# Second mixer's output for tokens 0-127 first, cross attention of tokens 128-255 behind the first key scores

## The reference

```python
x = x + merged @ w_out[l]                                  # "wo2"
h = rmsnorm(x, norm_xa_g[l]); m = rmsnorm(mem, norm_mem_g[l])
x = x + memory_cross_attention(h, m, xa_w_q[l], xa_w_kv[l], xa_w_o[l])   # "xq", "xo"; 4 heads of 128, 256 memory rows
h = rmsnorm(x, norm_ffn_g[l])
x = x + peer_ffn(h, peer_w_q[l], peer_subkeys[l], peer_w_down[l], peer_w_up[l])   # "pq", experts
return rmsnorm(x, final_g)
```

## Time and profile before

| | us |
|---|---|
| median of 3 runs | 1304.25 |
| lowest, highest | 1302.63, 1304.44 |
| span of the profiled execution | 1302.2 |
| median less that span | 2.05 |
| TensorE busy | 1188.0 (91%) |
| VectorE busy | 920.6 (71%) |
| ScalarE busy | 545.5 (42%) |
| first gather issued | 642.48 |

### The profile page before, as it was taken

The page is one execution under the profiler, slowest core; times in us unless marked ns, Lnnn a source line. Parts: engine busy times, 40 slices in busy tenths (PEclk is TensorE's granted clock), DMA queues, the critical chain, the costliest instruction groups (busy, mean ns, idle before and its releaser), DMA issues.

```text
span 1302.2 us, 16734 instructions
## 1 busy us (share of the span) xinstructions
PE 1188.0 (91%) x5950; PEld 845.7 (65%) x5950; DVE 920.6 (71%) x1836; ACT 545.5 (42%) x983; POOL 285.0 (22%) x261
## 2 busy tenths in 40 slices
PE   9999999999999999999999889999777877777776
PEld 9998999888888999998865545545322332332322
DVE  6885858777854865567797777776767777777655
ACT  5833655566533547536643333322322222222312
POOL 0000000000000000000145455443643444544420
PEclk9999999999999999999999999999999999989999
DMA  7544456455655654456799999999999999999996
GB/s 287 194 166 148 167 200 213 169 178 183 225 195 194 213 176 160 164 196 230 318 408 402 420 419 420 419 420 419 420 420 418 421 419 422 419 422 419 420 420 262
DMA packets 55925, 396.67 MB, mean 305 GB/s; under 512 B 6320, under 2 KB 6320, under 8 KB 8624
## 3 DMA queue, kind: packets, MB, share of 16 engines
q0 software_dynamic: 36864, 268.45, 49.9%
q1 hardware_dynamic: 17136, 119.16, 25.6%
q10 hardware_dynamic: 1856, 8.13, 1.8%
HBM read 394.67 MB, written 1.05 MB: 304 GB/s over the span
## 4 chain that ended last, share of the span: by engine, by line
PE 56%; DMA 31%; DVE 6%; issue 3%; ACT 3%; POOL 2%; DVEq 0%; POOLq 0%; ACTq 0%
DMA R<-experts,IDX 31%; PE ps L606 19%; PE ps L707 10%; PE ps L1190 8%; PE ps L926 4%; PE ps L654 3%; PE ps L928 2%; POOL R L2778 2%; PE ps L618 2%; DVE R L2564 2%; PE ps L674 1%; PE ps L1041 1%; PE ps L1095 1%; ACT DIAG L1645 1%; PE ps L1068 1%
## 5 line engine op out<-in xcount | busy, mean ns | idle before, releaser
L1190 PE MATMUL ps<-R,DIAG 128*128 128x512 f32 x1020 | 484.6, 623 | 102.7 <-ACT DIAG L1645 97.5
L1190 PEld LDWEIGHTS ps<-R,DIAG 128*128 128x128 f32 x1020 | 191.5, 197 | 371.3 <-issue 206.9
L2564 DVE CUSTOM_DVE_ANT_0 R<-R,XN 128x1024 f32<-128x1024 f32 x256 | 313.4, 1227 | 143.5 <-DMA R<-experts,IDX 137.8
L2778 POOL DMA_INDIRECT R<-experts,IDX x256 | 283.7, 1108 | 535.4 <-PE ps L1190 278.4
L1774 DVE TENSOR_TENSOR w_lo<-raw,w_hi 128x1024 fp32r<-128x1024 f32 x204 | 241.7, 1220 | 89.3 <-ACT w_hi L1243 84.9
L1243 ACT ACTIVATE w_hi<-raw 128x1024 fp32r<-128x1024 f32 x203 | 204.7, 1051 | 78.0 <-DMA raw<-weights 78.0
L1633 ACT ACTIVATE act_d<-dots,rst 128x2 f32<-128x2 f32 (+1 forms) x130 | 38.5, 296 | 329.4 <-DVE dots L2564 329.2
L1645 ACT ACTIVATE DIAG<-con,coef 128x128 f32<-128x128 f32 x255 | 88.6, 394 | 121.3 <-DVE coef L2573 118.1
L606 PE MATMUL ps<-both_C,w_hi 128*128 128x256 f32 x576 | 105.3, 284 | 0.3 <-ACT GA L1277 0.3
L2758 POOL TENSOR_SCALAR_AFFINE_SELECT WS<-WS 128x1024 f32<-128x1024 f32 x1 | 1.1, 1085 | 439.0 <-DMA BS<-gbs 439.0
L606 PEld LDWEIGHTS ps<-both_C,w_hi 128*128 128x128 f32 x576 | 90.3, 192 | 1.4 <-issue 0.8
(11 more groups left out here) (407 smaller groups left out, 1734.2 us busy)
## 6 DMA issues: line engine op xcount, KB each, us to landing
raw<-weights SPq DMA_DIRECT2D x103, 1024.0 KB, 4.8
PQW<-weights SPq DMA_DIRECT2D x6, 1024.0 KB, 9.4
R<-experts,IDX POOLq DMA_INDIRECT x256, 31.8
LNR<-rows ACTq DMA_DIRECT2D x3, 1024.0 KB, 4.7
raw<-weights SPq DMA_DIRECT2D x4, 512.0 KB, 8.4
XF<-xT SPq DMA_DIRECT2D x2, 512.0 KB, 5.6
MEM<-mem ACTq DMA_DIRECT2D x1, 1024.0 KB, 5.0
XR<-x ACTq DMA_DIRECT2D x1, 1024.0 KB, 7.8
```

The costliest lines, as they stand in the source:

```text
L1190: mm = pe.matmul(psum[:, 4 + 2 * m + n, :], DIAG[:, k, :], rows_[:, D + n * 512:D + (n + 1) * 512], start=(it % 8 == 0 and k == 0), stop=True,
L2564: dve.tensor_tensor_reduce(out=rows_[:, 0:D], in0=rows_[:, 0:D], in1=XN[:, m, :], scale=1.0, scalar=0.0, op0=ALU.mult, op1=ALU.add, accum_ ...
L2778: pool.indirect_dma_start(out=R[u][:, :], out_offset=None, in_=experts, in_offset=bass.IndirectOffsetOnAxis(ap=IDX[:, it, k:k + 1], axis=0 ...
```

## The change

What it does, part by part:

- **wo2.** Its first two blocks are loaded early into free buffers and split there, so that all four blocks lie in SBUF at once. TensorE computes both column halves for tokens 0-127 first (`wo2_rows`), and tokens 128-255 in pieces (`second`) between the steps of the first half's cross attention.
- **Norms.** The rows are transposed without the gain; the evacuation from PSUM multiplies by it. The root mean square of the cross attention's norm goes into the scale of the softmax's exponential. The second half's query is computed in its transposed form.
- **Cross output of tokens 0-127.** Its second block is computed in two groups of 256 columns.
- **Cross attention of tokens 128-255** starts behind `head_scores(0, 0)`. Its query and its output are plain fp32 matmuls on weights that are loaded a second time (`XQB`, `XOB`).
- **Queries.** All eight `pq` blocks have buffers of their own; the first query is written in two banks and evacuated in two pieces.
- **Buffers.** The first eight gathers have other buffers, opened by other events. VectorE, before the first dots, has the gains of half 0 and the second half's softmax; the residuals of half 1 come in the first pass, with waits for the cross output.

```diff
-        OPENED = {0: (11, None), 1: (18, None), 2: (8, VALUES_END)}
...
+        OPENED = {0: (18, ("xo_a", 3)), 1: (6, ("xo_a", 3)), 2: (2, ("xo_a", 3)), 3: (11, ("xq_b", 1)),
+                  4: (12, ("xq_b", 1)), 5: (8, ("values", 1)), 6: (1, ("xo_b", 2)), 7: (5, ("xo_b", 2))}
...
+            load(ma + 1, slot_of(ma + 1), half_end(ma - 3))
+            whole(early_raw[0], wo2, early_in[0])
+            load(gm, slot_of(gm), half_end(ma - 2))
+            sp.wait_ge(gm_ready, 2)
+            whole(early_raw[1], wo2 + 1, early_in[1])
...
             sp.wait_ge(m2_ready, 4)
...
+            for j in range(3):
+                whole(PQW[j], PQ0 + j, pq_in[j])
+            sp.wait_ge(xq_a, 1)
+            load(xo, slot_of(xo))
+            sp.wait_ge(xq_a, 2)
+            load(xo + 1, slot_of(xo + 1))
+            sp.wait_ge(gemm_done, half_end(wo2))
+            whole(XQB[0], xq, xqb_in[0])
+            sp.wait_ge(gemm_done, half_end(wo2 + 3))
+            whole(XQB[1], xq + 1, xqb_in[1])
+            for j in range(3, 8):
+                whole(PQW[j], PQ0 + j, pq_in[j])
+            sp.wait_ge(xo_a, 1)
+            for g in range(2):
+                whole(XOB[g], xo + g, xob_in[g])
...
+            def cross_query_second():
...
+                for h in range(XH):
+                    for k in range(DC):
...
+                        mm = pe.matmul(bank(r)[:, h * P:(h + 1) * P],
+                                       XQB[k // 4][:, at_, (h % 2) * P:(h % 2 + 1) * P], H3B[:, k, :],
+                                       start=(h == 0 and k == 0), stop=(k == 7), skip_group_check=True)
+                mm.then_inc(xq_b, 1)
...
+            def cross_out_second(g):
+
+                pe.wait_ge(xob_in[g], 16)
+                for i in range(4):
+                    mm = pe.matmul(psum[:, 6 + g, :], AXB[:, i, :],
+                                   XOB[g][:, 2 * i:2 * i + 2, :].rearrange("p a b -> p (a b)"),
+                                   start=(i == 0), stop=(i == 3), skip_group_check=True)
+                mm.then_inc(xo_b, 1)
...
+            turn("h3Tc", 0, "wo2", 4, XR, 1, range(4, 8))
+            head_scores(0, 0)
+            cross_query_second()
             cross_scores(1, 0)
             cross_scores(1, 1)
-            turn_side("h4Ta", 1, 0, 1, 6)
-            query(0, 0)
+            query(1, 0)
             cross_turn(1, 0)
-            head_scores(0, 0)
             cross_turn(1, 1)
-            query(1, 0, (0,))
             cross_values(1)
-            query(1, 0, (1,))
             head_scores(1, 0)
-            has_lo(pe, *values_parts(1))
-            side("xo", AXo, 0, 1)
-            side("xo", AXo, 1, 1)
-            query(2, 0)
+            query(2, 0, (0,))
+            wait_aux(pe, "xpvb")
+            cross_out_second(0)
+            cross_out_second(1)
+            query(2, 0, (1,))
             query(3, 0, (0,))
             head_scores(2, 0)
...
             first_eight()
-            values_lo(1)
             inverse_side(3, 0)
+            dve.wait_ge(rows2_in, 16)
+            gain_side(0, first_cols)
+            gain_side(0, last_cols)
             second_eight()
+            cross_max(1, 0)
+            cross_max(1, 1)
             top_h(0)
-
+            cross_weights(1, 0)
+            cross_weights(1, 1)
+            dve.wait_ge(xn_gain, 2)
+            dot_rows(0, 0)
             top_a(1)
-            top_b(1)
-            dot_rows(0, 0)
-            residual_side("xo", 3, 1, 0)
             coefs(0, 0)
             dot_rows(0, 1)
-            residual_side("xo", 4, 1, 1)
+            top_b(1)
             coefs(0, 1)
-            gain_side(1, 1, 0)
-            gain_side(1, 1, 1)
+            residual_side("xo", 4, 1, first_cols)
+            residual_side("xo", 5, 1, last_cols)
+            gain_side(1, first_cols)
+            gain_side(1, last_cols)
             top_c(1)
             dot_rows(0, 2)
```

More of the change, by code:

```diff
@@ L69, in half_end, with slot_of, split_end @@
     return 2 * b + h + 1
+EARLY = (BLOCK["wo2"], BLOCK["wo2"] + 1)
+SLOT = {BLOCK["wo2"] + 2: 3, BLOCK["wo2"] + 3: 0, BLOCK["xq"]: 1, BLOCK["xq"] + 1: 2, BLOCK["xo"]: 1,
+        BLOCK["xo"] + 1: 2}
+LOADED = {}
+for _n in range(BLOCK["wo2"]):
+    LOADED[_n] = _n // 4 + 1
+for _n, _s in SLOT.items():
+    LOADED[_n] = 1 + max(v for b, v in LOADED.items() if SLOT.get(b, b % 4) == _s)
+def slot_of(b):
+    return SLOT.get(b, b % 4)
+def split_end(b, h=1):
+    return half_end(b if b < BLOCK["wo2"] else b - 2, h)
 def group_end(stage, j):
@@ L659, in by_rows, with query_part @@
                             mm.then_inc(gemm_done, 1)
+            def query_part(j, m, c, ks):
+                r = RING["pq"] + QUERIES.index((j, m))
+                apart = (j, m) == (0, 0) and c == 1
+                dst = bank(r + 1 if apart else r)[:, c * P:(c + 1) * P]
+                for k in ks:
+                    mm = pe.matmul(dst, PQW[j][:, k, c * P:(c + 1) * P], H4[m][:, k, :],
+                                   start=((c == 0 or apart) and k == 0), stop=(k == 7), skip_group_check=True)
+                return mm
@@ new lines, in wo2_rows @@
+            def wo2_rows(g, m, i):
+                k, h = i // 4, i % 4 // 2
+                w = wo2_weights(g, k, h)
+                if m == 0:
+                    has_lo(pe, "m2", i // 2)
+                for n, (a, o) in enumerate(parts(w, opC)):
+                    mm = pe.matmul(psum[:, 4 + 2 * m + g, :], o[:, i, m * P:(m + 1) * P],
+                                   a[:, 2 * (i % 4):2 * (i % 4) + 2, :].rearrange("p a b -> p (a b)"),
+                                   start=(i == 0 and n == 0), stop=(i == 7 and n == 2), skip_group_check=True)
+                if m == 0 and i == 7:
+                    mm.then_inc(wo2_a, 1)
+                elif m and i % 2:
+                    mm.then_inc(gemm_done, 1)
@@ new lines, in _, with second, turn @@
+            second_rows = iter([(g, i) for g in range(2) for i in range(8)])
+            def second(count):
+                for _ in range(count):
+                    g, i = next(second_rows)
+                    wo2_rows(g, 1, i)
+            def turn(name, j, stage, n, src, m, chunks):
+                dst = free_aux(name, j)
+                wait_wide(pe, stage, n)
+                for n_, c in enumerate(chunks):
+                    mm = pe.transpose(dst[:, n_ * P:(n_ + 1) * P], src[:, m, c * P:(c + 1) * P], ident)
+                mm.then_inc(aux_done, 1)
@@ L1150, in _ @@
+            turn("h3Ta", 0, "wo2", 1, XR, 0, range(4))
+            for i in range(4, 8):
+                wo2_rows(1, 0, i)
+            cross_query(0, 0)
+            turn("h3Ta", 1, "wo2", 2, XR, 0, range(4, 8))
+            cross_query(0, 1)
+            cross_query(1, 0)
+            cross_query(1, 1)
+            second(1)
+            wait_drained(pe, "xq", 0)
+            transposes("qTa", 0, [QN[:, h * P:(h + 1) * P] for h in range(XH)])
+            second(1)
             cross_scores(0, 0)
@@ L1264, in ahead @@
             def ahead(b):
-                while split_to[0] < min(b, BLOCK["pq"] - 1):
+                while split_to[0] < min(b, BLOCK["wo2"] - 1):
                     split_to[0] += 1
@@ L2604, in _ @@
             coefs(0, 4)
-            rows_across("h4Tb", 1)
+            rows_across(1)
             top_h(1)
```

636 lines of the change are left out of this document (323 added, 313 removed).

## The result

The changed kernel takes 1311.19 us (median of 5 runs, 1310.72 to 1312.79) against 1304.25 before: ratio 1.0063, 95% interval 1.0052 to 1.0073, so slower by 0.5 to 0.7%. Forecast were 1310.5 us and "slower". The profiled execution has a span of 1309.0 us against 1302.2.

A forecast was written before the change was run, and what follows sets the result against it. TensorE was taken to bound the kernel up to the first sum, the gathers' transfers after it. Work +3.0 and waits +3.9 us delay that sum; between +4.4 and +7.8, +6.3 was taken: 1304.25 to 1310.5 us, range 1301.5 to 1314.0.

The forecast's parts named there:

- The bound: TensorE bounds up to the first sum; gathers at 420 GB/s later carry a delay at about 700 us to the end.
- Early projections cost nothing: Before the first sum: early wo2 split, reordered residuals and gains in evacuations cost nothing, hidden on VectorE and ScalarE.
- First gather: Work removed ahead of the first key scores, 8.1 us, moves the first gather from 642.48 to about 634.4 us.
- TensorE's work: Before the first sum: fp32 cross query +1.87, cross output +1.44, half-width groups +0.15, query transposes -0.45; sum +3.0 us.
- TensorE's waits: Second half's cross attention, a chain through three engines: 5.4 us of waits against 1.5 idle before, +3.9 us.
- First sum and ninth gather: First sum at 665.7 us; ninth gather waits for the second sum, issued at 669.6, landing +7.8 us later.
- The hole: After five gathers in flight and the sixth at about 652 us, the DMA idles some 8 us before later gathers.
- the gathers never dry up: Rival, faster: buffers six to nine free before the DMA empties at 655 us; about -5.5, 1298.7 us; chance 0.13.
- So TensorE sets the pace again: Behind the ninth gather, up to the 24th: TensorE sets the pace, +6.9 us; DMA's possible return makes +4.4 at most.
- The table loads: ScalarE's three table reloads before the fifth sum's diagonals, 1.78 us of TensorE's idle time, would recur 6.9 us later.
- TensorE doesn't wait: Rival, no change: handovers hide, first sum at 661.8 us, end moves +0.5 to 1304.8 us; chance 0.2.
- Starves longer: Rival, slower still: pass 0's dots and diagonals queue behind late residuals, DMA loses another 3 us; +9.5, 1313.7 us; chance 0.17.

The follow-up runs named there:

- b_more_pe: Kernel before plus eight plain fp32 matmuls of 512 columns ahead of the second half's cross output: 1311.85 us, ratio 1.0063.
- a_again: The changed kernel unaltered, measured a second time in another group of runs: 1313.25 us, ratio 1.0081.
- a_weights_first: Changed kernel with VectorE's two products of the second softmax ahead of the last part of the first pick list: 1311.23 us, ratio 1.0054.
- a_sum_best: Changed kernel with the first two sums around the second cross output's second half and VectorE's softmax weights earlier: 1311.58 us, ratio 1.0058.
- b_sum_first: Kernel before with the first sum ahead of a query and key scores, its VectorE products and ScalarE diagonals also earlier: 1307.8 us, ratio 1.0030.
- a_tables_early: Changed kernel with ScalarE's square root and next gate's exponential, hence the table loads, ahead of the fourth activation: 1311.18 us, ratio 1.0061.
- a_waits_out: Changed kernel with softmax products, last normed chunks and half a query earlier, first two gather buffers exchanged: 1310.41 us, ratio 1.0055.
- a_sum_first: Changed kernel with the first sum directly behind the second half's cross output, ahead of two queries and key scores: 1312.74 us, ratio 1.0071.
- b_tables: Kernel before with ScalarE's gelu and diagonals of the fifth pair ahead of its table reloads: 1304.94 us, ratio 1.0014.

## Why the prediction was right, point by point

**The bound.** Right in kind. The transfers behind 720 us run at 420 GB/s in both kernels, so a delay at 700 us is kept, and the delay comes from TensorE. b_more_pe shows that work on TensorE alone makes such a delay. The forecast calls TensorE the bound up to the first sum; in the kernel before the chain of waits runs through VectorE from 640.50 to 671.12 us, but for 0.3 us of ScalarE, so VectorE is about as near to being the bound there.

**Early projections cost nothing.** Nearly. In front of the first key scores TensorE waits 0.65 us for H3A's low part and 0.17 for the query's, counted in the forecast as 0.5 for "small ones". That the projections' order is otherwise free was read from the trace only; no experiment undid it.

**First gather.** Forecast 634.4, measured 632.73 and 634.59 (a_again). Both are 48.2 and 50.3 us behind the start of the second projection, which itself shifts by up to 2.0 us from one execution to another, in kernels of either order; I take no part of it for the change.

**TensorE's work.** Forecast +3.0 us, and its terms hold: the second cross query takes 7.38 us with its tail (forecast 7.3 and the tail), the second cross output 6.87 (forecast 6.88). The busy time of the stretch grew by 4.8 us, and the rest of it, 1.8 us, was not forecast: the same 16 matmuls of the values take 3.25 us in the changed kernel and 1.95 before, and the four of the key scores 1.06 and not 0.6, at half the clock.

**TensorE's waits.** Forecast 5.4 us (its terms add up to 5.5), measured 5.58. One by one: normed rows 0.98 (1.2), cross query's copy 0.84 (0.8), softmax weights 1.83 and none (1.8 and 0.4), copy of the turned weights 0.89 (0.8), small ones 0.82 (0.5), with 0.2 left over. a_weights_first shows that the 1.8 were VectorE's order.

**First sum and ninth gather.** Forecast 665.7 and 669.6; measured 666.24 and 670.61 (668.10 and 672.47 in a_again). The first figure profits from an execution that begins 1.3 us earlier, which hides most of the slow clock. Measured from the second projection, the sum comes 8.9 us later (81.83 against 72.98), not 6.9.

**The hole.** Forecast: five gathers in flight, the sixth at 652, then 8 us without transfers. Measured: the sixth at 653.15, seven and eight at 662.66 and 663.90 (forecast 661.8). The rate is below 420 for longer than forecast, as the ninth to twelfth gather come thinly as well. Against that stand 4.19 MB moved between 640 and 650 us, where it was 2.16. The balance of 640 to 680 us is 2.84 MB or 6.8 us. The rival in which the gathers never dry up fell with this.

**The number, and luck in it.** The forecast had +7.8 us for the ninth gather's landing and let the transfers win back up to 3.4 us of it. By bytes the shift is 8.2 us at 680 us and 6.8 at 700, so something is won back, 1.3 us. More than that wasn't there to win: by its rates (409 GB/s from 660 to 680, 392 from 680 to 700 us) the kernel before loses 1.9 us in that stretch and not 3.4, as the forecast counts the ninth gather by bytes and the 24th by its landing. The +6.3 was picked between +4.4 and +7.8 and not worked out; that it comes so near 6.9 is in part luck, and the second measurement has 10.0.

**Two steps that were wrong, though the number wasn't.** The first is that the ninth gather carries the delay: "the ninth gather waits for the second sum (3.44 us for two) and not for the first". This wait is real, but a_sum_best brings the ninth gather to 667.77 and b_sum_first to 657.62, and neither gains from it. In these two later sums wait for diagonals (1.17 and 2.41 us), and in a_sum_best the seventh and eighth gathers come later. What carries the delay are all of TensorE's steps that gathers 6 to 15 wait for, up to 680 us. The second is "So TensorE sets the pace again" behind them, with the table loads' wait 6.9 us later: from 680 us on the changed kernel's transfers run at 420 GB/s, so they set the pace there, and a_tables_early has its 24th gather 3.4 us earlier for nothing. The forecast held since the gathers around the ninth are as late as it is: the seventh and eighth come 8.2 us later than before, the ninth 9.0, the twelfth 7.3.

**The table loads.** "would recur 6.9 us later": 2.31 us ahead of the fifth sum in place of 1.78, at 685.55 in place of 678.25, 7.3 us later. The wait recurs as said, but at a point where it costs the changed kernel nothing.

**The other rivals.** "TensorE doesn't wait" fell with 5.58 us of waits. "Starves longer" had its price in a_again (10.0 us against 9.5), but not its mechanism: TensorE computes the first four sums from 666.24 us without a wait, so dots and diagonals hold nothing up there. The two measurements, 6.9 and 10.0 us, leave open whether the true loss lies nearer the forecast or this rival.

**Left open.** How much of the loss is work, how much waits and how much the slow clock can't be split cleanly: of the waits that were removed a part came back elsewhere. By the table, of 8.7 us more up to the 40th gather 4.0 are busy and 4.7 idle time. A version with the cross output of tokens 128-255 in three parts (less work, but the second loads' buffers and splitting) wasn't tried, nor was a_waits_out together with a_tables_early, which aim at the stretches ahead of and behind 680 us.

## What to carry to other kernels

Where one engine's queue feeds a stream of transfers that is full from some point on, compare, stretch by stretch up to that point, how many bytes are left, and look at what each transfer waited for in the stretches where it is short. Starting the first transfers earlier, or one consumer earlier, wins nothing that could be told here, as later ones stayed behind that queue; and an earlier step wins nothing once the stream is full. Pulling a chain of small steps through three engines close together costs its handovers, here 5.6 us where 1.5 stood before, and shuffling one engine's order won back 2.8 us of the 3.9 to 5.8 expected. A constant distance seen in eight traces is not a cause: it took a kernel that moved the first sum to break it.

## What the runs showed of the hardware

**TensorE's clock.** In the changed kernel the granted clock is 0.83 on the mean of 650 to 660 us, where it was 1.00 before: for a third of that time it is at the lower of its two levels, 1.2 GHz. Ahead of it TensorE was busy for 7.13 of 10 us, with waits of 1.83 and 0.89 us. a_again has 0.83 there too. The same waits stand in a_sum_first, whose order is the same up to that point, and there the values take 2.02 us and the granted clock of 646 to 653 us is 1.00, so it doesn't come each time.

```profile
647.20 1.46 PE L1159 MATMUL ps<-con,XS 128*128 128x128 f32 x8 [1.83 <-DVE XS L2476]
649.54 2.02 PE L1170 MATMUL ps<-XT,VX 128*128 128x128 f32 x16 [0.89 <-ACT XT L1672]
```

It falls in the same way at single sums: 5.40 us in place of 3.6 or 3.7 behind waits of 2.31 and 2.41 (b_sum_first), 2.14 (b_more_pe) and 2.77 us (a_tables_early), with a granted clock of 0.72 to 0.76 in the 6 or 7 us around them, while the changed kernel's 2.31 us are followed by a sum of 3.70 at 1.00. So a wait of 2 us can cost 1.8 us more behind it, and whether it does differs from one execution to another. The Trainium skill, TensorE: Matmul & The Clock Gate, section "HAM oscillation — how this bites in real kernels", has idle gaps between bursts of matmuls throw the clock back to half. The traces here agree in kind (the falls stand behind waits of 1.8 to 2.8 us) and add that not every such wait is followed by one.

**Plain fp32 against three parts.** At 512 columns an fp32 matmul took 0.86 us (6.87 for 8) and three fp32r parts 0.68 (5.44 for 24), so the split saves a fifth of TensorE's time, for which ScalarE pays 1.05 us and VectorE 1.22 us for each 128x1024 numbers of a weight.

**Table loads.** Each took 1.28 us. Three close together stood behind a wait of TensorE of 1.78 us (before), 2.31 us (changed) and 1.54 us (b_tables); in a_tables_early, where they lie apart, behind 0.90 us.
